# Four RWKV norm items between the output tiles, one sequence of norm buffers, HGRN squares one tile ahead

## The reference, cut to what matters

```python
# RWKV half: y has 8 heads of 64, both directions added
y = y[0] + jnp.flip(y[1], axis=1)
y = ((y - mean) * lax.rsqrt(var + LNX_EPS)).reshape(B, T, D_RWKV)
y = y * lnx_w + lnx_b
y_a = (y + bonus * v) * g
# HGRN half: chunks of a scan with a state, both directions added
S = exp(G_last) * S + einsum(k_c * exp(G_last - G), v_c)
o = o[0] + jnp.flip(o[1], axis=1)
o = o * lax.rsqrt(jnp.mean(o * o, axis=-1, keepdims=True) + HGRN_NORM_EPS) * gnorm_w
y_b = o * silu(gate)
# output projection, residual, second norm, then the router and the experts
x = x + concat([y_a, y_b]) @ w_out
h2 = _rms_norm(x, norm2_w)
x = x + _hier_moe(h2, ...)
```

## Time and profile before

| | us |
|---|---|
| median of 3 runs | 2429.05 (2422.94 to 2430.99) |
| the profiled execution | 2425.25 |
| its span in the trace | 2423.6 |
| TensorE's mean granted clock, as a share of full speed | 0.968 |

### The profile page before, as it was taken

How to read it: one execution, slowest core, us unless ns; L and a number is a source line. 1 busy time by engine, 2 the same in 40 slices (tenths; PEclk the granted TensorE clock), 3 DMA queues, 4 the chain that set the end, 5 groups by cost and what they waited for, 6 DMA issues and landing times. The chain is left out here.

```text
span 2423.6 us, 64805 instructions
## 1 busy us (share of the span) xinstructions
PE 2266.9 (94%) x28110; PEld 1485.1 (61%) x28110; DVE 1028.8 (42%) x2175; ACT 719.3 (30%) x1446; POOL 418.3 (17%) x520
## 2 busy tenths in 40 slices
PE   7989999989999999999968888995899999999997
PEld 4444544445555555555556656753788888888883
DVE  3236777634745645645645645543111111111115
ACT  4224554534544534534512312221000000000003
POOL 1002222200000000000012100012433334333331
PEclk9999999999999999999969988997899999999999
DMA  4113343533342432432366733251899999999986
GB/s 137 35 49 130 133 153 122 190 71 90 90 125 65 117 99 69 121 95 68 109 193 179 214 111 102 92 184 48 325 360 358 332 360 332 357 331 357 363 308 227
DMA packets 359836, 436.48 MB, mean 180 GB/s; under 512 B 164896, under 2 KB 296112, under 8 KB 351408
## 3 DMA queue, kind: packets, MB, share of 16 engines
q1 hardware_dynamic: 343232, 397.94, 48.2%
q0 software_dynamic: 14256, 35.04, 5.9%
q10 hardware_dynamic: 2112, 0.01, 0.1%
HBM read 329.87 MB, written 102.93 MB: 179 GB/s over the span
## 5 line engine op out<-in xcount | busy, mean ns | idle before, releaser
L1161 PE MATMUL h_pp<-hT,r_wcol 128*128 128x512 f32 x832 | 414.1, 621 | 9.1 <-ACT h_iraw L1289 9.1
L2715 PE MATMUL e_ps_gu<-e_xT,e_wg 128*128 128x128 f32 x2048 | 236.6, 277 | 18.3 <-DVE e_xT L2790 18.3
L2715 PEld LDWEIGHTS e_ps_gu<-e_xT,e_wg 128*128 128x128 f32 x2048 | 233.8, 194 | 18.8 <-DVE e_xT L2790 18.8
L2715 PEld LDWEIGHTS e_ps_gu<-e_xT,e_wu 128*128 128x128 f32 x2048 | 233.7, 192 | 14.8 <-issue 14.8
L2715 PE MATMUL e_ps_gu<-e_xT,e_wu 128*128 128x128 f32 x2048 | 233.9, 275 | 0.0
L2724 PE MATMUL e_ps_y<-e_wd,e_hid 128*128 128x512 f32 x512 | 225.1, 593 | 1.1 <-DVE e_hid L2804 1.1
L1161 PEld LDWEIGHTS h_pp<-hT,r_wcol 128*128 128x128 f32 x832 | 142.1, 190 | 130.2 <-issue 109.2
L500 PE MATMUL h_pp<-hT,r_wcol 128*128 128x512 f32 x480 | 209.0, 593 | 1.3 <-DVE hT L770 1.3
L2797 DVE TENSOR_SCALAR e_y<-e_ps_y,e_row 128x512 f32<-128x512 f32 x32 | 24.0, 750 | 336.0 <-PE e_ps_y L2724 336.0
L2724 PEld LDWEIGHTS e_ps_y<-e_wd,e_hid 128*128 128x128 f32 x512 | 95.0, 191 | 108.3 <-issue 108.3
L500 PEld LDWEIGHTS h_pp<-hT,r_wcol 128*128 128x128 f32 x480 | 90.3, 190 | 109.7 <-issue 108.0
(11 more groups left out here) (374 smaller groups left out, 3456.8 us busy)
## 6 DMA issues: line engine op xcount, KB each, us to landing
e_wg<-in_moe_w_gate_dram SPq DMA_DIRECT2D x32, 2048.0 KB
e_wu<-in_moe_w_up_dram SPq DMA_DIRECT2D x32, 2048.0 KB, 14.6
e_wd<-in_moe_w_down_dram SPq DMA_DIRECT2D x32, 2048.0 KB
r_wcol<-in_w_in_dram SPq DMA_DIRECT2D x35, 512.0 KB, 5.3
ar<-r_ar SPq DMA_DIRECT2D x24, 512.0 KB, 2.7
kb<-r_kb SPq DMA_DIRECT2D x24, 512.0 KB, 2.8
m_ar<-ar SPq DMA_DIRECT2D x48, 256.0 KB, 4.7
m_kb<-kb SPq DMA_DIRECT2D x48, 256.0 KB, 3.5
```

The lines of the kernel that those rows point to most:

```text
L1161: last = nc.tensor.matmul(pp[n % 2][:], wcol[(k + 2) % 3][:, c], self.hT[:, c, span(s)], start=c == 0, stop=c == KT - 1)
L2715: last = nc.tensor.matmul(ps[:, q * P:(q + 1) * P], w[u][:, c, q * P:(q + 1) * P], xT[u][:, c * P:(c + 1) * P], start=c == 0, stop=c == KT ...
```

## The change

The last four RWKV norm items (8 to 11) leave the run at the start and stand between the entries of output tiles 0 to 3. Both kinds of item get one sequence `SEQ` of buffer positions, in the order in which they now come: r0 to r7, h0, r8, h1, r9, h2, r10, h3, r11, h4, then h5 to h11. `num(p)` is the item at position p, and `sq`, `var`, `wide` and the gate buffers go by p. The HGRN square `n_sq` of item n + 2 now follows `n_wide` of item n + 1. VectorE's `n_ss` gets a wait for ScalarE's `wide` of two positions before, where that was an HGRN item. SP loads the second half of `w_out` at RWKV items 4 to 7 (before: 8 to 11), clears the slots at item 6 (8) and loads the router's weights at item 7 (9).

```diff
+        LEAD = 8
+        SEQ = [("r", k) for k in range(LEAD)] + [("h", 0)]
+        for n in range(1, TILES):
+            SEQ += [("r", LEAD + n - 1)] * (LEAD + n - 1 < ITEMS) + [("h", n)]
+        UNITS = len(SEQ)
...
-                for i in range(ITEMS + 5):
...
+                def more(name, k, cost=0.0):
+                    if LEAD <= k < ITEMS:
+                        out.append((name, (at["r", k] if name[0] == "n" or name == "r_gate" else k,), cost, 0))
...
                 norm("n_sq", 0)
                 norm("n_ss", 0, 0.9)
+                more("n_sq", LEAD)
                 norm("n_inv", 0)
+                more("n_ss", LEAD)
                 norm("n_wide", 0, 1.1)
+                norm("n_sq", 1)
                 for n in range(TILES + 1):
-                    norm("n_sq", n + 1)
+                    k = LEAD + n
+                    more("r_sum", k + 1)
+                    more("r_next", k)
+                    more("n_inv", k)
                     late("h2n", n - 1, 0)
                     if n >= EARLY:
                         late("half", n, 3.5, 0, 0)
                     norm("n_ss", n + 1, 0.9)
                     route("choose", n, 0)
                     late("turn", n - 1, 1.1, 0)
...
                     norm("n_inv", n + 1)
                     late("half", n, 3.5, 0, 1)
+                    more("n_wide", k, 1.1)
+                    more("n_sq", k + 1)
                     norm("n_wide", n + 1, 1.1)
+                    norm("n_sq", n + 2)
                     route("choose", n, 1)
...
+                    more("r_gate", k)
                     late("turn", n - 1, 1.1, 1)
                     late("half", n, 3.5, 1, 1)
+                    more("n_ss", k + 1)
                     late("x1", n, 0)
                     late("routed", n - 1, 1.7)
...
                     def n_ss(k):
                         r = var[k % 2]
+                        if k >= 2 and not is_r(k - 2):
+                            self.waits(eng, act_wide.at("wide", num(k - 2)))
```

More of the change, by code:

```diff
@@ L1760, in goes_to, with g_full @@
                 return t, t < mirror(t) if d else t > mirror(t)
+            def g_full(p):
+                return g_loaded[p % RING_G], sum(32 if is_r(q) else 16 for q in range(p % RING_G, p + 1, RING_G))
             def summed(t):
@@ L1775, in fillers, with lead, early @@
                 out = []
-                for i in range(ITEMS + 5):
[L1777 to L1791, removed]
-                ready = lambda n: max(FINISHED[n], mirror(FINISHED[n])) if n < TILES else 0
+                at = {item: p for p, item in enumerate(SEQ)}
+                ready = lambda n: max(FINISHED[n], mirror(FINISHED[n])) if n < TILES else 0
+                def lead(name, k, cost=0.0):
+                    if 0 <= k < LEAD + (name == "r_sum"):
+                        out.append((name, (k,), cost, -1))
+                def early(name, n, cost, *more):
+                    if 0 <= n < EARLY:
+                        out.append((name, (n,) + more, cost, -1))
                 def norm(name, n, cost=0.0):
                     if n < TILES:
-                        out.append((name, (ITEMS + n,), cost, ready(n)))
+                        out.append((name, (at["h", n],), cost, ready(n)))
+                def more(name, k, cost=0.0):
+                    if LEAD <= k < ITEMS:
+                        out.append((name, (at["r", k] if name[0] == "n" or name == "r_gate" else k,), cost, 0))
                 def late(name, n, cost, *more):
@@ L2053, in r_next @@
                                     sp.dma_start(dst, w).then_inc(params, 16)
[L2054 to L2057, removed]
+                    schedule(scores=scores, out=out, scanned=scanned, x1=x1, r_next=r_next, r_load=r_load, r_gate=lambda p: load_g(p + RING_G),
+                             n_wide=lambda p: None if is_r(p) else load_g(p + RING_G),
                              turn=lambda n, h: store_h2(n) if h == 0 else load_x(n + RING_X) if n + RING_X >= EARLY else None)
@@ L2197, in n_ss @@
                         r = var[k % 2][:, 0:2 * PAIRS if is_r(k) else PAIRS]
-                        self.waits(eng, dve_var.at("var", k) if is_r(k) else bank_y.done(("ss", k)))
+                        self.waits(eng, dve_var.at("var", num(k)) if is_r(k) else bank_y.done(("ss", k)))
                         nc.scalar.activation(r, r, ACT.Sqrt).then_inc(*act_root.inc("root"))
@@ L2331, in n_ss @@
                         else:
-                            self.waits(eng, bank_y.full(("ss", k)), act_wide.ago("wide", k - ITEMS, 2))
+                            self.waits(eng, bank_y.full(("ss", k)))
                             nc.vector.tensor_scalar(r[:, 0:PAIRS], ps_y[:, 0:PAIRS], 1.0 / P, EPS_H, ALU.mult, ALU.add
```

79 lines of the change are left out of this document (47 added, 32 removed).

## The result

The changed kernel takes 2446.4 us (median of 8 runs, 2439.3 to 2454.9), the kernel before 2429.2 in the same session (2422.9 to 2435.2): a ratio of 1.0071, 95% interval 1.0055 to 1.0086, which is 17 us slower. The forecast was 2439, slower, with a range to 2449. The profiled execution took 2443.17 us (span 2441.6), against 2425.25 before.

A forecast was written before the change was run, and what follows sets the result against it. TensorE, busy for 94% of the span, was taken as the bound, losing time by standing or half clock. Standing +13.5, clock -3 and GpSimd +0.5 gave +11, taken as +10: 2439 us by the median 2429.05, range 2418 to 2449.

The forecast's parts named there:

- terms 1 to 9: Waits of TensorE up to tile 5 in the new order: 42.2 us in all, against 28.7 before, +13.5.
- 9: Tile 4 waits 1.5 us (before 2.03) and tile 5 waits 2.7 (before 0), behind prep of step 10.
- the clock: Loss to half clock of 15 to 19 us, mean 17, for 20 before: -3 us, bounds 10 and 24.
- The start of step 10: Scan step 10 begins near 1555 instead of 1545.0, and behind it both traces run alike.
- GpSimd: GpSimd's adds beside VectorE's prep slow its products by 1.07 us where they meet: +0.5 us, bounds 0 and 4.
- term 1: At HGRN item 0 TensorE waits 0.7 us for the square and 5.5 for the scale, together 6.2.
- Term 8: At tile 3 msq, place and h2n stand behind prep of step 9: 6.3 us wait, before 2.04 + 1.12.
- gives back only about an n_ss: Squaring one tile ahead alone saves about an n_ss (0.9 us) at each of five places.
- rival C: Slower still: earlier w_out loads delay a gate or keys, 2444 us; sign: longer stretch before 1371; chance 0.08.
- D: The budget cuts off the square ahead, or kinds wait for each other's buffers: 2439 us too; no chance given.
- B: No change: stands near 34 us instead of 42, the clock loses 15, 2429 us; chance 0.22.
- Rival A: Faster: VectorE reaches x1 of tiles 0, 1 and 3 as early as before: -10 us, 2419; chance 0.20.

The follow-up runs named there:

- dvebank_nosq: Kernel after with squares where they stood before, and the moved items' r_gate behind h2n, n_wide and n_inv placed elsewhere; 1.0039 of the kernel before.
- fill: Kernel after with idle matmuls in five of TensorE's stands; 1.0025 of the kernel before.
- fill_before: Kernel before with idle matmuls where its TensorE stood; 0.9947 of the kernel before.
- fill_all: Kernel after with idle matmuls in nearly all its stands between scan steps 6 and 9; 1.0017 of the kernel before.
- sq_before: Kernel before with only the HGRN squares one tile ahead; 1.0024 of the kernel before.
- hold: Kernel after, but a square not yet due is stepped over so that due entries behind it run; 1.0040 of the kernel before.
- lead12: Kernel after with no RWKV item moved; squares ahead, one sequence of buffers and earlier loads kept; 1.0028 of the kernel before.
- lead10: Kernel after with only RWKV items 10 and 11 moved; 1.0062 of the kernel before.
- nosq: Kernel after with each HGRN square where it stood before, so only the items move; 1.0032 of the kernel before.

## Why the prediction was right, and where it wasn't

**The time.** 2446.4 against 2439 and a range to 2449: slower, as forecast, and further out than my middle by 7 us. Part of that nearness is luck: at equal work the standing came out 2.3 us under its term and the busy time 10.6 over, and the two misses work against each other.

**The standing, terms 1 to 9.** The sum was 42.2, of which 39.9 were measured: +11.2 instead of +13.5. 1: forecast 6.2, measured 0.61 + 7.34. 2: 5.2, measured 1.68 + 1.73 + 1.69. 3: 2.6, measured 1.20 + 1.22. 4: 7.0, measured 6.90. 5: 3.95, measured 0.93 + 1.10 + 1.53. 6: 4.35, measured 1.70 + 2.45. 7: 2.35, measured 2.42. 8: 6.3, measured 4.81 + 0.31. 9: 4.2, measured 1.87 + 0.41. Following the order through the queues, gap by gap, gave six of the nine terms here to within 0.4 us, and 1, 8 and 9 to within 2; within 9, tile 5 has 0.41 where 2.7 were forecast.

**The step that was off is the clock.** I took -3 us, "a loss of 15 to 19, mean 17, for 20 before". It came to +7.6: the same 1967 records are busy 303.4 us instead of 295.8, so that the loss is nearer 28 than 17, above its bound of 24. The reason that I gave was that long stands lie further apart and those of 1.0 to 1.8 us may do nothing. They don't do nothing. In the kernel after some 31 us of half clock lie at its three stands over 4 us (7.34, 6.90, 4.81), about as much again at stands of 1.2 to 2.5 us, and 7 in steps 10 and 11; in the kernel before some 27 lie at its stands of 3.9 us and more and 17 at those of 2.03 (read from windows of 0.5 us). dvebank_nosq stands no longer than before and its instructions take 9 us more, and with the stands filled 11 to 13 us come back in fill, fill_before and fill_all. So many shorter stands kept the clock down as a few long ones did. The Trainium skill ("TensorE: Matmul & The Clock Gate", section "A second HAM failure mode: psum-queue depth-cycling") tells of a kernel in which short but frequent idle times between groups of matmuls let the clock swing between its two levels. It gives them no size and no price; this trace agrees in kind, with half clock after a stand of 1.87.

**The start of step 10.** I named 1555; it is 1551.4, although all that the terms hold is there. About 9 us of work (second halves of tile 6, turn and routed of tile 5) had moved behind step 11, so that at equal work it is 15 us behind. The prediction has this move in its terms and forgot it in its sign: by its own sum step 10 had to begin near 1546, and that 1551.4 lies close to 1555 is luck. Then steps 10 and 11 take 26.80 us instead of 23.46, at a clock of 0.87 instead of 1.00, with no stand over 1.22, and of that size and place in both kernels. These 3.3 of the 7.6 us no stand explains. That both traces run alike holds only behind the last step of the scan, where after too has full clock (1578.2 to 1678.0: 1.00).

**GpSimd.** +0.5 was taken, bounds 0 and 4. VectorE of the kernel after, in prep of step 6:

```profile
1371.44 1.55 DVE L2309 TENSOR_TENSOR g_k<-e_wg,g_decay 128x256 f32<-128x256 f32 x1
1372.91 1.75 DVE L2312 TENSOR_TENSOR e_wg<-e_wg,g_to 128x512 f32<-128x512 f32 x1
1374.59 1.21 DVE L2315 TENSOR_TENSOR e_wd<-e_wg,g_to 128x1024 f32<-128x1024 f32 x1
```

and GpSimd beside it:

```profile
1371.44 1.27 POOL L1971 TENSOR_TENSOR o_spare<-o_spare,o_x 128x512 f32<-128x512 f32 x1
1372.66 1.45 POOL L1965 TENSOR_TENSOR y<-y,o_ob 128x512 f32<-128x512 f32 x1
```

The two products take 0.42 and 0.69 elsewhere, so 2.2 us went in prep, in the chain that TensorE waited for: enough for the 1.75 by which term 1 was short. No run moves the adds alone, so this is read from the rows and not tested. By the rule of the Trainium skill ("SBUF — State Buffer", section "Who interferes with whom") a product with two inputs in SBUF may have to stand for the whole of an add; the trace agrees, with 1.13 and 1.06 us lost beside adds of 1.27 and 1.45.

**What I put down to the wrong part.** Term 8, right in size, comes from the squares' due time and not from the moved items (sq_before and hold). So the sentence that squaring ahead alone "gives back only about an n_ss" at each of the five places was wrong in sign: by the runs with and without, it costs 6 us in the kernel before and 9 in the kernel after. lead12 minus sq_before leaves 0.0004 for the earlier loads and the one sequence, less than the two can tell (some 0.002); but the stretch ahead hasn't become longer (the scores of step 4 at 1333.58 and 1333.61), which was rival C's sign, so C is out. So is D: the wait for the square fell from 12.1 to 1.8 us. B, no change, is out by the interval: the standing is 39.9 where it had 34, and the clock cost more and not less. Rival A, "VectorE being free in time", would have been 5 us of standing less than before and 4 to 5 us back from the clock; dvebank_nosq, which mends VectorE's order, has the standing of before and loses 9 in busy time. What two moved items already cost (lead10) and why its busy time is the longest of the kernels without idle matmuls (306.4) is shown as a size, not explained.

## What to carry to other kernels

Count stands and slower instructions apart, in a window with the same number of instructions on both sides: if the busy time of equal work grows, the order costs by the clock, and shorter waits alone won't bring it back. In a list that is taken in order and stops at the first entry not yet due, an entry that costs nothing can still hold back all others when it is moved ahead; look at its due time. Where the waits can't be removed, try to fill them: idle matmuls in nine stands of the kernel before gave 0.5%, more than any of the reorderings tried.

## What the runs showed of the hardware

Stands of TensorE under 2.5 us were followed by half clock in some places and not in others. The kernel after, around its stand of 1.87 us (ahead of 1523.30), and where it stands for 1.69 and 1.10 us (ahead of 1458.73 and 1461.35):

```profile
1519.00:1530.00 11.00, 9.13 (x39) 5.84 (x39) 4.18 (x14) 2.12 (x5) 0.00 (x0) 0.69 0.49 145
1455.00:1472.00 17.00, 14.22 (x165) 11.81 (x163) 10.59 (x19) 5.25 (x12) 0.00 (x0) 1.00 0.37 109
```

Half clock also came where TensorE didn't stand at all. Behind the scores of scan step 4, ahead of every changed instruction and with TensorE busy throughout, the kernel before and fill_before:

```profile
1335.00:1347.00 12.00, 12.00 (x78) 9.33 (x78) 8.44 (x16) 5.38 (x13) 1.08 (x1) 1.00 0.80 257
1335.00:1347.00 12.00, 12.00 (x71) 10.02 (x71) 8.44 (x16) 4.31 (x11) 1.70 (x1) 0.86 0.85 272
```

nosq, sq_before and fill have 0.86 there too. Steps 10 and 11 of the kernel after, with half clock, hold the same stands of 1.22 us that they hold in the kernel before at full clock. So the stands are not the whole of it, and what decides at a given place stays open. Filling them took most of the half clock away all the same: 13 us are left in the windows of fill_before and of fill_all, where the unfilled kernels have 46 and 69.

One execution isn't another, even in code that is the same. The scores of the same scan step, well ahead of every change, in before and in hold:

```profile
1263.03 1.92 PE L2078 MATMUL o_ps_s<-e_wg 128*64 128x32 f32 x16
```

```profile
1270.14 1.12 PE L2110 MATMUL o_ps_s<-e_wg 128*64 128x32 f32 x16
```

hold is 7.1 us behind here, ahead of its first moved entry. A difference of spans between two profiles holds that too, and the windows of equal work leave it out.
